# Moving the weight slots of a matmul kernel through eight 64-byte places, with all activations on multiples of 512 bytes

## The reference

```python
u = jnp.take(expert_down, ec, axis=0)
hdn = jax.nn.gelu(jnp.einsum('ted,td->te', u, xc))
vsel = jnp.take(expert_up, ec, axis=0)
return jnp.einsum('te,ted->td', gc * hdn, vsel)
```

## Time and profile before

| what | value |
|---|---|
| time, median of 3 | 2786.56 us |
| the profiled execution's own time | 2786.72 us |
| its span, first to last instruction | 2784.8 us |
| TensorE busy | 2768.7 us, 99%, 14898 matmuls |
| weight loads busy (overlap matmuls) | 2371.7 us |
| VectorE, ScalarE, GpSimd busy | 1821.0, 1410.8, 742.8 us |
| mean granted TensorE clock | 0.999 |
| DMA | 559.01 MB, mean 201 GB/s |

### The profile page before, as it was taken

How to read it: one execution, slowest core, us unless ns; L and a number is a source line. 1 busy time by engine, 2 the same in 40 slices (tenths; PEclk the granted TensorE clock), 3 DMA queues, 4 the chain that set the end, 5 groups by cost and what they waited for, 6 DMA issues and landing times.

```text
span 2784.8 us, 38959 instructions
## 1 busy us (share of the span) xinstructions
PE 2768.7 (99%) x14898; PEld 2371.7 (85%) x14898; DVE 1821.0 (65%) x2878; ACT 1410.8 (51%) x2001; POOL 742.8 (27%) x411
## 2 busy tenths in 40 slices
PE   9999999999999999999999999999999999999998
PEld 7887888888888888888888888888888888999886
DVE  6567667877777655555555555666777876555555
ACT  5455654555555544444444444546655555444454
POOL 0012200388888888810000000001202111000000
PEclk9999999999999999999999999999999999999999
DMA  8654478878777777777767677775665556666664
GB/s 274 208 165 135 148 254 301 270 192 190 190 193 193 189 191 192 193 220 222 216 216 223 214 237 228 227 212 189 188 177 158 160 153 196 190 190 190 189 199 156
DMA packets 199017, 559.01 MB, mean 201 GB/s; under 512 B 53344, under 2 KB 69872, under 8 KB 195888
## 3 DMA queue, kind: packets, MB, share of 16 engines
q1 hardware_dynamic: 161744, 556.04, 65.5%
q0 software_dynamic: 36944, 0.41, 2.8%
q10 hardware_dynamic: 144, 0.07, 0.0%
HBM read 535.32 MB, written 21.12 MB: 200 GB/s over the span
## 4 chain that ended last, share of the span: by engine, by line
PE 96%; DVE 2%; ACT 1%; issue 1%; DMA 0%; SPq 0%; POOL 0%; DVEq 0%; ACTq 0%
PE bank L549 95%; PE bank L561 1%; DVE wlo L960 1%; ACT whi L1724 1%; DMA VV<-in_xT 0%; DVE QKb L963 0%; ACT aX L1724 0%; ACT L1724 0%; DVE AT L1225 0%; DVE tmpc L963 0%; ACT DD L1724 0%; DVE HB L963 0%; DVE lbs L1234 0%; DVE tmpc L1568 0%; ACT scr L1724 0%
## 5 line engine op out<-in xcount | busy, mean ns | idle before, releaser
L960 DVE TENSOR_TENSOR wlo<-raw,whi 128x1024 fp32r<-128x1024 f32 (+1 forms) x965 | 1193.3, 1238 | 841.4 <-ACT whi L1724 837.7
L1724 ACT ACTIVATE whi<-raw 128x1024 fp32r<-128x1024 f32 (+1 forms) x967 | 1017.5, 1055 | 989.6 <-PE bank L549 977.9
L549 PE MATMUL bank<-aX,whi 128*128 128x512 f32 (+1 forms) x4000 | 970.1, 392 | 0.0
L549 PE MATMUL bank<-whi,aX 128*128 128x512 f32 x2944 | 911.3, 390 | 0.9 <-DVE aX L963 0.5
L549 PEld LDWEIGHTS bank<-aX,whi 128*128 128x128 f32 (+1 forms) x4000 | 726.1, 187 | 144.4 <-issue 3.7
L549 PEld LDWEIGHTS bank<-whi,aX 128*128 128x128 f32 x2944 | 552.3, 188 | 119.5 <-DVE aX L963 1.8
L1684 POOL DMA_INDIRECT gate_scratch<-gate,place x256 | 584.1, 2282 | 247.6 <-DMA gate_scratch<-HB 169.3
L549 PE MATMUL bank<-wlo,aX 128*128 128x512 f32 x1472 | 572.0, 390 | 1.4 <-DVE wlo L960 1.4
L549 PEld LDWEIGHTS bank<-aX,wlo 128*128 128x128 f32 (+1 forms) x3984 | 501.1, 187 | 22.3 <-issue 0.5
L549 PE MATMUL bank<-aX,wlo 128*128 128x256 f32 (+1 forms) x3984 | 515.8, 279 | 0.2 <-DVE wlo L960 0.2
L549 PEld LDWEIGHTS bank<-wlo,aX 128*128 128x128 f32 x1472 | 276.2, 188 | 59.9 <-DVE wlo L960 2.7
(11 more groups left out here) (233 smaller groups left out, 1903.5 us busy)
## 6 DMA issues: line engine op xcount, KB each, us to landing
raw<-in_w_down SPq DMA_DIRECT2D x256, 512.0 KB, 3.8
raw<-in_w_up SPq DMA_DIRECT2D x256, 512.0 KB, 4.3
raw<-in_w_in SPq DMA_DIRECT2D x176, 512.0 KB, 3.7
raw<-in_w_out SPq DMA_DIRECT2D x32, 512.0 KB, 4.0
gate_scratch<-HB SPq DMA_DIRECT2D x16, 1024.0 KB, 7.4
raw<-in_w_pq SPq DMA_DIRECT2D x32, 512.0 KB, 5.3
raw<-in_w_o SPq DMA_DIRECT2D x32, 512.0 KB, 4.3
raw<-in_w_pg SPq DMA_DIRECT2D x32, 512.0 KB, 3.9
```

Source lines behind the costliest of these rows:

```text
L549: return e.matmul(o, lhsT, rhs, start=start, stop=stop, skip_group_check=True)
L960: e.tensor_tensor(wlo[:, s, 0:n], raw[:, r, 0:n], whi[:, s, 0:n].bitcast(F32), ALU.subtract).then_inc(s_lo, 1)
L1724: return e.activation(o, i, f, **k)
```

## The change

`whi` and `wlo` become flat tensors of three slots and 128 spare elements. A function `place_of(u)` gives the offset of a unit within its slot, in elements: 16 elements, 64 bytes, for each step. In the down stage it starts at 0 and rises by one step every 30 units up to 7; in the up stage it starts at 7 and falls by one every 30 units to 0; in all other stages it is 0. Two units whose slots overlap are kept apart by `last_over(u)`: ScalarE waits for the last earlier unit that overlaps. `aM` becomes `aX`, and `aX` loses its 128 spare elements.

```diff
-    whi = alloc(ctx, "whi", [128, NSPL, UNIT], F32R)
-    wlo = alloc(ctx, "wlo", [128, NSPL, UNIT], F32R)
-    aXs = alloc(ctx, "aX", [128, 16 * 512 + 128], F32R)
+    whis = alloc(ctx, "whi", [128, NSPL * UNIT + 128], F32R)
+    wlos = alloc(ctx, "wlo", [128, NSPL * UNIT + 128], F32R)
+    aXs = alloc(ctx, "aX", [128, 16 * 512], F32R)
     aX = aXs[:, 0:8192].rearrange("p (k c) -> p k c", k=16)
-    aM = aXs[:, SHIFT:SHIFT + 8192].rearrange("p (k c) -> p k c", k=16)
+    aM = aX
...
+    def place_of(u):
+
+        if DOWN0 <= u < UP0:
+            return 16 * min((u - DOWN0) // 30, 7)
+        if UP0 <= u < UP1:
+            return 16 * max(7 - (u - UP0 + UP0 % 3) // 30, 0)
+        return 0
+
+    def start_of(u):
+        return u % NSPL * UNIT + place_of(u)
+
+    def last_over(u):
+        return next(v for v in range(u - 1, -1, -1) if abs(start_of(v) - start_of(u)) < UNIT)
+
+    def whi(u, a, z):
+        return whis[:, start_of(u) + a:start_of(u) + z]
...
-                        last = mm(o, whi[:, s, k * 128:k * 128 + 128], ax[:, row(kt), :], kt == 0, final and k == 7)
+                        last = mm(o, whi(u, k * 128, k * 128 + 128), ax[:, row(kt), :], kt == 0, final and k == 7)
...
                 if u >= NSPL:
-                    w.wait_ge(s_mm, u - NSPL + 1)
-                act(whi[:, s, 0:n], raw[:, r, 0:n], ACT.Copy).then_inc(s_hi, 1)
+                    w.wait_ge(s_mm, last_over(u) + 1)
+                act(whi(u, 0, n), raw[:, r, 0:n], ACT.Copy).then_inc(s_hi, 1)
```

More of the change, by code:

```diff
@@ L389, in _build, with wlo @@
     PQ0 = G["pq", 0].first
+    def place_of(u):
[10 more added lines that the diff above has]
+        return whis[:, start_of(u) + a:start_of(u) + z]
+    def wlo(u, a, z):
+        return wlos[:, start_of(u) + a:start_of(u) + z]
     ROUTE = {PQ0 + 11 + (16 * c + k if c < 2 else 34 + 24 * (c - 2) + 3 * k // 2): (c, k) for c in range(8) for k in range(16)}
@@ L708, in unit_x @@
                     if high:
-                        last = mm(o, whi[:, s, k * 128:k * 128 + 128], ax[:, row(kt), :], kt == 0, final and k == 7)
+                        last = mm(o, whi(u, k * 128, k * 128 + 128), ax[:, row(kt), :], kt == 0, final and k == 7)
                     else:
-                        last = mm(o[:, 256:512], wlo[:, s, k * 128:k * 128 + 128], ax[:, row(kt), 0:256], False, False)
+                        last = mm(o[:, 256:512], wlo(u, k * 128, k * 128 + 128), ax[:, row(kt), 0:256], False, False)
             last.then_inc(s_mm, 1)
@@ L729, in group_f @@
                     ready(kt)
-                    mm(o, whi[:, s, c], xh[:, kt, :], kt == 0, False)
-                    mm(o, whi[:, s, c], xl[:, kt, :], False, False)
+                    mm(o, whi(u, c.start, c.stop), xh[:, kt, :], kt == 0, False)
+                    mm(o, whi(u, c.start, c.stop), xl[:, kt, :], False, False)
                     w.wait_ge(s_lo, u + 1)
-                    last = mm(o, wlo[:, s, c], xh[:, kt, :], False, u == g.end - 1 and k == 7)
+                    last = mm(o, wlo(u, c.start, c.stop), xh[:, kt, :], False, u == g.end - 1 and k == 7)
                 last.then_inc(s_mm, 1)
@@ L747, in group_t @@
                         ts = slice(t * 128, t * 128 + 128)
-                        mm(bs[t], xh(kt)[:, ts], whi[:, s, c], kt == 0, False)
+                        mm(bs[t], xh(kt)[:, ts], whi(u, c.start, c.stop), kt == 0, False)
                         w.wait_ge(s_lo, u + 1)
-                        mm(bs[t], xh(kt)[:, ts], wlo[:, s, c], False, False)
-                        last = mm(bs[t], xl(kt)[:, ts], whi[:, s, c], False, u == g.end - 1 and k == 1)
+                        mm(bs[t], xh(kt)[:, ts], wlo(u, c.start, c.stop), False, False)
+                        last = mm(bs[t], xl(kt)[:, ts], whi(u, c.start, c.stop), False, u == g.end - 1 and k == 1)
                 last.then_inc(s_mm, 1)
@@ L825, in first_units @@
                         if high:
-                            mm(bs[t], ax_hi(kt)[:, ts], whi[:, u, c], kt == 0, False)
+                            mm(bs[t], ax_hi(kt)[:, ts], whi(u, c.start, c.stop), kt == 0, False)
                         else:
-                            last = mm(bs[t], ax_hi(kt)[:, ts], wlo[:, u, c], False, False)
+                            last = mm(bs[t], ax_hi(kt)[:, ts], wlo(u, c.start, c.stop), False, False)
                     if high:
@@ L832, in first_units @@
                             ts = slice(t * 128, t * 128 + 128)
-                            mm(bs[t], ax_lo(kt)[:, ts], whi[:, u, c], False, False)
+                            mm(bs[t], ax_lo(kt)[:, ts], whi(u, c.start, c.stop), False, False)
             last.then_inc(s_mm, 1)
@@ L852, in _ @@
             c = slice(kt * 16, kt * 16 + 16)
-            mm(o, whi[:, s, c], aX[:, kt, 0:256], kt == 0, False)
-            mm(o, whi[:, s, c], aX[:, kt, 256:512], False, False)
-            last = mm(o, wlo[:, s, c], aX[:, kt, 0:256], False, kt == 15)
+            mm(o, whi(u, c.start, c.stop), aX[:, kt, 0:256], kt == 0, False)
+            mm(o, whi(u, c.start, c.stop), aX[:, kt, 256:512], False, False)
+            last = mm(o, wlo(u, c.start, c.stop), aX[:, kt, 0:256], False, kt == 15)
         last.then_inc(s_mm, 1)
@@ L893, in _ @@
                     o = vacant(UPF[k]) if i == 0 else banks[UPB[k]]
-                    mm(o, wring[:, i % NW, c], whi[:, s, f], i == 0, False)
-                    mm(o, wring[:, i % NW, c], wlo[:, s, f], False, False)
-                    last = mm(o, wring[:, i % NW, 256 + t * 128:384 + t * 128], whi[:, s, f], False, i == 127)
+                    mm(o, wring[:, i % NW, c], whi(u, f.start, f.stop), i == 0, False)
+                    mm(o, wring[:, i % NW, c], wlo(u, f.start, f.stop), False, False)
+                    last = mm(o, wring[:, i % NW, 256 + t * 128:384 + t * 128], whi(u, f.start, f.stop), False, i == 127)
             last.then_inc(s_mm, 1)
@@ L938, in _ @@
                 c = slice(kt * 512, kt * 512 + 512)
-                mm(bs[t], pH[:, kt, ts], whi[:, s, c], kt == 0, False)
-                mm(bs[t], pH[:, kt, ts], wlo[:, s, c], False, False)
-                last = mm(bs[t], pL[:, kt, ts], whi[:, s, c], False, kt == 1)
+                mm(bs[t], pH[:, kt, ts], whi(u, c.start, c.stop), kt == 0, False)
+                mm(bs[t], pH[:, kt, ts], wlo(u, c.start, c.stop), False, False)
+                last = mm(bs[t], pL[:, kt, ts], whi(u, c.start, c.stop), False, kt == 1)
             last.then_inc(s_mm if t else s_pt, 1)
@@ L959, in split @@
                 w.wait_ge(s_hi, u + 1)
-                e.tensor_tensor(wlo[:, s, 0:n], raw[:, r, 0:n], whi[:, s, 0:n].bitcast(F32), ALU.subtract).then_inc(s_lo, 1)
+                e.tensor_tensor(wlo(u, 0, n), raw[:, r, 0:n], whi(u, 0, n).bitcast(F32), ALU.subtract).then_inc(s_lo, 1)
         def tt(o, a, b, op):
@@ L1943, in _ @@
                 w.wait_ge(s_raw[u], 16)
-                act(whi[:, u, 0:512], raw[:, u, 0:512], ACT.Copy).then_inc(s_h0, 1)
-                act(whi[:, u, 512:1024], raw[:, u, 512:1024], ACT.Copy).then_inc(s_hi, 1)
+                act(whi(u, 0, 512), raw[:, u, 0:512], ACT.Copy).then_inc(s_h0, 1)
+                act(whi(u, 512, 1024), raw[:, u, 512:1024], ACT.Copy).then_inc(s_hi, 1)
             if kt in (7, 11):
```

## The result

The changed kernel takes 2805.3 us (median of 4, 2805.01 to 2806.6) where the kernel before takes 2786.64 (median of 4): a ratio of 1.0069, 95% interval 1.0057 to 1.0081, so 18.7 us slower. The forecast was 2810, with a range from 2789 to 2825.

A forecast was written before the change was run, and what follows sets the result against it. TensorE's matmul start-to-start interval was taken to bound the kernel. Terms 5.3 - 1.3 + 0.8 + 7.4 + 11.6 = +23.8 us on 2786.72 gave about 2810 us, range 2789 to 2825.

The forecast's parts named there:

- What bounds the kernel: Whole kernel: TensorE busy 99% of the span; time is matmul count times start-to-start interval, and only the interval can move.
- the address distance decides: All matmuls: interval depends on d, moving minus stationary operand's byte offset modulo 512, in 64-byte steps; sum +23.8 us.
- each operand's own start: Rival: off multiples of 512, a stationary tile costs 6.7 ns, a moving one 2.5; +20.5 us, 2807 us; chance 0.08.
- no effect at all: Rival: addresses play no part and the interval stays as it was; 2787 us; chance 0.05.
- The ladder: Down and up stages: cost per matmul rises 0.7 ns a step, 2.5 at d = 1 to 6.7 at d = 7; chance 0.40.
- The up stage's +11.6: Up stage: weights move, place p gives d = p, seven places cost above the floor, place 0 free; +11.6 us.
- The down stage: Down stage: place 0 +0.8 us, place 7 unchanged, places 1 to 6 (d = 7 to 2) +7.4 us.
- The other stages: Outside down and up, the lost `aM` shift brings d to 0: +5.3 us for two-unit groups, -1.3 us for `iv`.
- The 104 groups: Two-unit groups outside the down stage with `aM` moving: d from 1 to 0, 5.517 to 5.567 us each, +5.3 us.
- New waits: Down-stage place changes: one unit at each waits for a nearer unit; taken as 0, possibly 0 to +6 us.
- neighbours only: Rival: d = 7, 0 and 1 cost what the trace shows, 2 to 6 nothing; +4.4 us, 2791 us; chance 0.16.
- full price: Rival: every middle distance costs the full 6.7 ns, only d = 0 and 1 cheap; +32.4 us, 2819 us; chance 0.26.

## Why the prediction was right, and where it was wrong

- **What bounds the kernel**: right. Only the interval moved.
- **That the address distance decides**: right, and by experiment: the same distance with both operands off gives the same unit times. The two rivals in which it does not, each operand's own start and no effect at all, are out. The first had +20.5 us, nearer to the measured +18.7 than the forecast's +23.8, and is wrong all the same: its number came near by chance. Nor is it the traffic of the other engines: in the down stage of the kernel before, VectorE's busy time falls from 78.95 us (800 to 900 us) to 56.68 (1000 to 1100 us), and TensorE has 581 matmuls in the one window and 582 in the other.
- **The rule cited in the prediction** from the Trainium skill, SBUF — State Buffer, "Who interferes with whom", has two independent read ports for TensorE. The runs do not agree with what the prediction drew from it, that placement has no price: a unit of the up stage takes 2.720 us at d = 0 and 2.800 at d = 7. Whether the two reads hold each other up, or something else that follows their distance, no run here shows.
- **The ladder** is the step that failed. It took a rise from d = 1 to d = 7 over 512 bytes. Measured in the up stage for d = 7 to 2: 6.7, 6.7, 2.2, 0, 6.7, 5.7, in sum 28.0 ns, where the ladder had 29.7. The mean is right and nearly every single value is not: in steps of 64 bytes the period is 256, so d = 7 was no far end but the value of d = 3 as well, and d = 4 is free. The up stage's +11.6 came out at +11.0 for that reason only.
- **The down stage** was given +8.2 and cost +5.7. The same ladder, and one assumption more: 256 columns were to be as dear as 512 at d = 7, and they are near their cheapest there, 113.6 ns, 0.3 above the floor and not 6.7. For d = 7 to 2 the 512 columns add up to 28.9 ns above the floor and the 256 columns to 19.9, where the ladder had 29.7 for each; so the miss is nearly all in the 256 columns. Place 0, +0.8, was right (2.783 us a unit).
- **The other stages**: `iv` -1.3 came out at -1.3. The 104 groups were given +5.3; the stages that hold them, with `ao` and `bo`, cost 3.8. A group does go from 5.517 to 5.567 where nothing interrupts it (`q2`, 8 groups, +0.4). But where score and recurrence matmuls stand between units the kernel before already ran dearer, at 116.7 ns for 256 columns in `cg` to `za` against 115.6 in the down stage, so there was less to lose: `cg` to `za` +0.5 where 32 groups were to cost 1.6. The 32 of `ga` and `gb` went the other way, +2.2 with `ao` and `bo` between them: 256 columns went from 115.6 to 119.5 ns, but 512 columns stayed at 229.3, where the prediction had them fall.
- **New waits**: 0 was right for the seven changes; TensorE waited as long as before. That they can cost was shown by the run with the step on slot 1: 4.6 us for one.
- Of the five middle places of the up stage the rival *neighbours only* was right for d = 4 (free), near for d = 5 (2.2 ns) and wrong for d = 2, 3 and 6. There *full price* was right, within 1.0 ns of its 6.7. Neither describes the whole, and the measured sum lies between the two.

The errors of the sums are -0.6 (up), -2.5 (down) and -1.5 (other stages), in all some 5 us of 24, because inside each sum the errors of single places cancel. That the sum came so near is in part luck. A forecast within 5 us of the result does not show that its mechanism is the right one; the view by blocks confirms the distance and refutes the ladder.

## What to carry to other kernels

When TensorE is always busy, compare the interval from start to start between stages of the same shape: a difference of 3% at the same clock pointed to the operands' addresses, and here of the distances tried a multiple of 256 bytes between moving and stationary operand was best where 512 columns of weights move, and 64 bytes (or 256 more) where activations of 512 and 256 columns alternate. Between two measured points don't draw a line before the period is known; a scan in blocks inside one run costs one kernel and gives the map. Where slots shift, step on a unit whose new place overlaps no unit in flight.

## What was not expected of the hardware

- The interval depends on the distance of the two operands with a period of 256 bytes: 2.720, 2.747, 2.789 and 2.800 us a unit in the up stage at 0, 64, 128 and 192 bytes, and again at 256 to 448, but for 2.800 at 384. The period is shown for multiples of 64 bytes alone. Why 256 stays open, as does why 64 bytes are cheaper than 16, 32 or 48.
- The state is handed on. In the up stage places 2 and 6 are the same distance modulo 256, and yet place 6 runs at a steady 2.800 us a unit and place 2 in a cycle from 2.780 to 2.795; whether the period is not exact there or the two blocks hold different states, no run tells. In the down stage of the kernel before the 512 columns have no single interval either: it goes 226, 229, 232 ns, over and over, and runs on so across units (the first two after a dear run of 256 columns are 234 and 236). The 256 columns run at 113.3 or 117.8 ns, mostly in turns. This is TensorE's timeline in the kernel before, near the start of the stage:

```profile
520.55 2.05 PE L549 MATMUL bank<-aX,wlo 128*128 128x256 f32 x16
522.43 3.83 PE L549 MATMUL bank<-aX,whi 128*128 128x512 f32 x16
...
542.70 1.98 PE L549 MATMUL bank<-aX,wlo 128*128 128x256 f32 x16
544.51 0.85 PE L549 MATMUL bank<-aX,whi 128*128 128x512 f32 x3
```

The two groups write the same PSUM bank (they are four groups apart, and four banks take turns) and have the same addresses but for the slot, yet the first run of sixteen takes 1.88 us and the second 1.81. What differs is the interval of the 512 columns just before: 229 ns before the first, 232 before the second. It is so in all unbroken runs of sixteen from `pq` to `za` in this kernel: the 94 that follow an interval of 225 to 230 ns run at 117.7 to 117.9, and of the 79 that follow one of 231 or 232, 77 run at 113.3 or 113.4, and the other two begin so, until a gap in their middle. In `pq`, with other matmuls between some units, 3 of 13 such runs are at 113.4, where in the down stage it is nearly every second: that fits the dearer 256 columns of such stages before the change, though no run tests it by itself.
- Even the best interval, 226.7 ns for 512 columns, is 6% over 213.3, which is what one column in each period of the 2.4 GHz clock would come to. No run here changed it.
